# Late modulation pieces on TensorE instead of VectorE, and gathers that pass over padding rows

## The reference, cut to what matters

```python
for layer in range(DEPTH):
    mod_l = jax.nn.silu(c) @ w_ada[layer] + b_ada[layer]        # 6 * 1024 values
    mod_c = jax.nn.silu(c_ctx) @ w_ada[layer] + b_ada[layer]
    sh1, sc1, g1, sh2, sc2, g2 = split(mod_l, 6)
    ...                                                         # mixer gives o_l, o_c
    x_lat = x_lat + g1 * o_l
    f_l = rms_norm(x_lat, g_ffn[layer]) * (1 + sc2) + sh2
    y = moe(f_l, w_router, b_router, w1[layer], w3[layer], w2[layer])
    x_lat = x_lat + g2 * y
```

## Time and profile before

| | us |
|---|---|
| three runs | 3264.39, 3264.18, 3256.47 |
| the profiled execution | 3262.42 |
| its span on the core | 3260.4 |
| TensorE matmul busy | 2899.2 (89%) |
| VectorE busy | 1555.3 (48%) |
| ScalarE busy | 1066.2 (33%) |
| GpSimd busy | 505.9 (16%) |
| mean granted TensorE clock | 0.943 of full |

### The profile page before, as it was taken

The page is one execution under the profiler, slowest core; times in us unless marked ns, Lnnn a source line. Parts: engine busy times, 40 slices in busy tenths (PEclk is TensorE's granted clock), DMA queues, the critical chain, the costliest instruction groups (busy, mean ns, idle before and its releaser), DMA issues. The chain is left out here.

```text
span 3260.4 us, 73070 instructions
## 1 busy us (share of the span) xinstructions
PE 2899.2 (89%) x27907; PEld 1918.0 (59%) x27907; DVE 1555.3 (48%) x4608; ACT 1066.2 (33%) x2418; POOL 505.9 (16%) x802
## 2 busy tenths in 40 slices
PE   6999986889998849999895999899998949997895
PEld 3777743845554437776683455477776526785683
DVE  2333346955557642222223688666666452222223
ACT  1111112456631103333232344355553202332232
POOL 0000002600033012232231000000002003232222
PEclk8999987989999969999997999899999969998998
DMA  9500046500044379999995222200002458999997
GB/s 344 209 26 26 13 182 248 134 1 1 1 144 168 123 312 417 415 417 417 418 400 179 84 91 71 78 1 1 1 1 86 160 226 334 417 416 417 418 416 308
DMA packets 163152, 661.79 MB, mean 203 GB/s; under 512 B 22388, under 2 KB 34852, under 8 KB 113764
## 3 DMA queue, kind: packets, MB, share of 16 engines
q1 hardware_dynamic: 132932, 564.32, 44.0%
q0 software_dynamic: 19424, 63.98, 5.3%
q10 hardware_dynamic: 10560, 30.16, 2.4%
HBM read 576.73 MB, written 81.66 MB: 202 GB/s over the span
## 5 line engine op out<-in xcount | busy, mean ns | idle before, releaser
L2637 PE MATMUL ps_g<-w_ring,work 128*32 128x256 f32 x9632 | 569.8, 384 | 37.5 <-DMA w_ring<-in_w 25.5
L2637 PEld LDWEIGHTS ps_g<-w_ring,work 128*32 128x32 f32 x9632 | 384.8, 111 | 184.7 <-issue 48.3
L2724 DVE STREAM_TRANSPOSE work<-work 128x256 f32<-128x256 f32 x189 | 123.9, 655 | 673.9 <-PE ps_g L2637 656.7
L2690 ACT COPY work<-ps_y 32x256 f32<-32x256 f32 x760 | 276.4, 364 | 285.9 <-PE ps_y L2652 279.1
L2652 PE MATMUL ps_y<-w_ring,work 128*32 128x256 f32 x4896 | 302.1, 380 | 3.3 <-ACT work L2690 3.3
L1771 PE MATMUL of_ps_r<-w_early,cat 128*128 128x512 f32 (+1 forms) x608 | 257.8, 580 | 3.0 <-ACT cat L1854 3.0
L430 PE MATMUL ps_r<-w,hT 128*128 128x512 f32 (+1 forms) x640 | 249.3, 546 | 1.5 <-ACT hT L489 1.5
L2652 PEld LDWEIGHTS ps_y<-w_ring,work 128*32 128x32 f32 x4896 | 202.7, 111 | 70.0 <-ACT work L2690 4.3
L2684 ACT ACTIVATE work<-ps_g 128x128 f32<-128x128 f32 x192 | 53.4, 278 | 542.4 <-PE ps_g L2637 535.8
L2596 POOL DMA_INDIRECT work<-f_dram,ex_idx x200 | 194.7, 974 | 157.4 <-POOL ex_idx L2593 155.9
L1771 PEld LDWEIGHTS of_ps_r<-w_early,cat 128*128 128x128 f32 x608 | 115.7, 194 | 127.1 <-issue 123.5
(11 more groups left out here) (494 smaller groups left out, 4268.0 us busy)
## 6 DMA issues: line engine op xcount, KB each, us to landing
w_ring<-in_w SPq DMA_DIRECT2D x304, 1024.0 KB, 26.5
w_early<-in_w SPq DMA_DIRECT2D x80, 1024.0 KB, 28.0
y_dram<-work ACTq DMA_DIRECT2D x190, 128.0 KB, 5.7
y_dram<-zeros POOLq DMA_DIRECT2D x2, 9216.0 KB, 44.6
ml_staging<-in_w_ada SPq DMA_DIRECT2D x9, 2048.0 KB, 11.9
mo_wa<-in_w_ada SPq DMA_DIRECT2D x6, 2048.0 KB, 9.4
ml_spare<-in_w_ada SPq DMA_DIRECT2D x5, 2048.0 KB, 13.3
ml_arena<-ml_rows SPq DMA_DIRECT2D x40, 256.0 KB, 4.3
```

Of the source, the lines that this page charges most:

```text
L2637: mm = pe.matmul(ps_h[rows, :], xT[:, k * UNIT:(k + 1) * UNIT], w[:, :, kk * DE + n * P:kk * DE + (n + 1) * P], start=k == 0, stop=k == KD ...
L2690: w = act.copy(y[b * UNIT:(b + 1) * UNIT, n * 256:(n + 1) * 256], ps_y[n * UNIT:(n + 1) * UNIT, :])
L2724: dve.transpose(xT.rearrange("p (k t) -> p k t", k=KD), xs.rearrange("p (r k) -> p k r", k=KD)).then_inc(x_turned, 1)
```

## The change

In the mix output of layer 0 the product of piece n moves from VectorE to TensorE: at the end of TensorE's iteration n, behind `router(n - 1)`, TensorE waits for the load of piece n and runs `ada_product` into the free half of `ps_c`. ScalarE copies the row into `M.gate`, rows that GpSimd has used up by then. Behind iteration N - 1 and ahead of `turn_f(N - 1)` TensorE turns all six rows back with 24 matmuls of two columns. VectorE adds the bias for both columns and makes the gain ahead of `scores(N - 2)`. SP's part is not changed: `ada_mm` is still what frees the buffer.

In `route` the values that form the list get an offset: every real entry is the same as before, and a place without a token becomes q - 4, which is negative, for its quarter q. The gather gets a bound (`bounds_check=T * QU - 1`, `oob_is_err=False`), so that such rows are passed over; their places in the tile keep what was there.

```diff
@@ mix_out, TensorE
-                    if 0 < n <= len(M.late):
-                        pe.wait_ge(ada_sum, n)
-                        for m in range(4):
-                            at = P + 4 * (n - 1) + m
-                            mm = pe.matmul(ps_r[:, at:at + 1], wa[:, 0, m * P:(m + 1) * P], g.ones[:, 0:1], start=True, stop=True)
-                        mm.then_inc(ada_mm, 1)
...
                     if n:
                         router(n - 1)
+                    if 0 < n <= len(M.late):
+                        pe.wait_ge(ada_in, 16 * n)
+                        if n > 1:
+                            pe.wait_ge(ada_row, n - 1)
+                        ada_product(pe, g, ps_c[:, 0, :], wa, ada_mm)
+                if M.late:
+                    pe.wait_ge(ada_row, len(M.late))
+                    for j in range(len(M.late)):
+                        for m in range(4):
+                            mm = pe.matmul(ps_c[:, 0, 8 * j + 2 * m:8 * j + 2 * m + 2], M.gate[:, j, m * P:(m + 1) * P], g.pick[:, :], start=True, stop=True)
+                    mm.then_inc(ada_turned, 1)
                 turn_f(N - 1)
@@ mix_out, ScalarE, at the end of iteration n
+                    if 0 < n <= len(M.late):
+                        act.wait_ge(ada_mm, n)
+                        act.wait_ge(normed, n)
+                        act.copy(M.gate[:, n - 1, :], ps_c[:, 0, :]).then_inc(ada_row, 1)
@@ mix_out, VectorE
-                def late(j):
-
-                    dve.wait_ge(ada_in, 16 * (j + 1))
-                    dve.tensor_scalar(wa[:, 0, :], wa[:, 0, :], g.cs[:, 0, 0:1], None, ALU.mult).then_inc(*c.up())
-                    for k in range(1, KD):
-                        own()
-                        w_sum = dve.scalar_tensor_tensor(out=wa[:, 0, :], in0=wa[:, k, :], scalar=g.cs[:, k, 0:1], in1=wa[:, 0, :], op0=ALU.mult, op1=ALU.add)
-                        w_sum.then_inc(*(c.up() if k < KD - 1 else (ada_sum, 1)))
...
-                    if 0 < n <= len(M.late):
-                        late(n - 1)
+                if M.late:
+                    dve.wait_ge(ada_turned, 1)
+                    at = slice(4 * M.late[0], 4 * M.late[-1] + 4)
+                    dve.tensor_tensor(g.mod[:, at, :], ps_c[:, 0, 0:8 * len(M.late)].rearrange("p (a w) -> p a w", w=2),
+                                      g.ba[:, at].unsqueeze(2).to_broadcast([P, 4 * len(M.late), 2]), ALU.add).then_inc(*c.up())
+                    own()
+                    ada_gain(dve, g, 1, 1).then_inc(*c.up())
                 scores(N - 2)
                 scores(N - 1)
@@ route
-    high = R.work[:, LOWS:LOWS + 2 * nt * LISTW]
+    high = R.work[:, 2 * nt * UNIT:2 * nt * (UNIT + LISTW)]
-                                           (tok[:, :], [[4 * P, nt]], 0, 4), (row_no[:, :], [[1, LISTW]], 0, 0)):
+                                           (tok[:, :], [[4 * P, nt]], QU, 4), (row_no[:, :], [[1, LISTW]], 0, 0)):
-            dve.memset(quarter[q * UNIT:(q + 1) * UNIT, :], float(q)).then_inc(*c.up())
+            dve.memset(quarter[q * UNIT:(q + 1) * UNIT, :], float(q - QU)).then_inc(*c.up())
@@ experts, gather
-                                    in_offset=bass.IndirectOffsetOnAxis(idx[:, at:at + 1].bitcast(U32), 0)).then_inc(gathered[at], 16)
+                                    in_offset=bass.IndirectOffsetOnAxis(idx[:, at:at + 1].bitcast(U32), 0),
+                                    bounds_check=T * QU - 1, oob_is_err=False).then_inc(gathered[at], 16)
```

More of the change, by code:

```diff
@@ L1349, in mix_out @@
         r_done, parts_out, l_done, lg_ready, lg_used = s("r_done"), s("parts_out"), s("l_done"), s("lg_ready"), s("lg_used")
-        ada_in, ada_sum, ada_mm = s("ada_in"), s("ada_sum"), s("ada_mm")
+        ada_in, ada_mm, ada_row, ada_turned = s("ada_in"), s("ada_mm"), s("ada_row"), s("ada_turned")
         ps_row = (ps_o[:, :], ps_c[:, :, :].rearrange("p a n -> p (a n)"))
@@ L2298, in route @@
     n, m = nt * NE, nt * NG
+    QU = P // UNIT
     fixed = FIXED
```

## The result

The changed kernel takes 3300.36 us (median of 4 runs, 3299.32 to 3302.13) against 3260.76 us for the kernel before on the same chip (median of 4, 3256.47 to 3264.39): 1.0123 times, interval 1.0105 to 1.014, or 39.6 us slower. The forecast was 3306 us, +43.

| stretch, from mark to mark | before | after | difference | forecast |
|---|---|---|---|---|
| up to output 1 of layer 0's mix output | 965.38 | 963.50 | -1.9 | 0 |
| output 1 to output 8 | 132.84 | 182.10 | +49.3 | +57 |
| output 8 to the first matmul of the routing | 56.33 | 56.99 | +0.7 | -1 |
| from there to the experts' first matmul | 38.79 | 39.68 | +0.9 | 0 |
| experts of layer 0 | 529.15 | 525.21 | -3.9 | -4.9 |

A forecast was written before the change was run, and what follows sets the result against it. TensorE bounds layer 0's mix output; in the experts TensorE and the DMA supply of weights lie close together. Stretch +57, turn -1 and gathers -13 give +43 us, about 3306 us, with a low end of 3291 and a high end of 3328.

The forecast's parts named there:

- The wait: Layer 0's mix output: TensorE waits 9.9 us for each load n = 2 to 6, none for n = 1.
- the rebuilt stretch: Output 1 to output 8 of layer 0's mix output, rebuilt from 16.40 us tiles: 189.8 us for 132.8, +57 us.
- The clock: Layer 0's mix output: lower TensorE clock behind each of five waits costs 2.9 us, between 1.7 and 4.2.
- The products: Layer 0's mix output: six products added to TensorE, 1.85 us each, 11.1 us at full clock, all on the path.
- The turn: End of layer 0's mix output: 48 records, 6.3 us, just fit TensorE's wait for the last `f`; taken as -1 us.
- The gathers: Experts of both layers: passed-over rows give DMA time back, 4.9 and 9.6 us, 14.5 together; 13 us taken.
- GpSimd: Start of each layer's experts, four gathers in a row: the bound's test taken as nothing, between -2 and +4 us.
- A: Experts: passed-over rows bring nothing, 3320 us; chance 0.16.
- B: Experts: gathers bring far more than their share, all 46.0 us of waiting for weights go, 3254 us; chance 0.02.
- C: Layer 0's mix output: whole wait hidden, only the products stay, stretch 125.9 us, 3243 us; chance 0.02.
- D: Experts: each gather gets longer on GpSimd; at +1 us, 3314 us; chance 0.08 together with longer waits.

The follow-up runs named there:

- products alone: The changed kernel with the gathers of before, so only the products have moved: 3315.02 us, 1.0157 times the kernel before.
- gathers alone: The kernel before with only the gathers changed: 3247.52 us, 0.9958 times the kernel before.
- one-tile-later kernel: The changed kernel with each product one iteration later on TensorE, and ScalarE's copy with it: 3243.23 us, 0.9934 times the kernel before.

## Why the prediction was right

The mechanism was right: five waits in the predicted place decide, and the gathers give part back. That the total came out so close, +43 against +39.6, is partly luck: the stretch of the mix output was 7.7 us less than forecast, and the gathers and the turn, each 1.7 us worse, took nearly half of that away again.

*The wait.* Right in place, count and cause: none for the first product, five for the others, each the 0.5 us and the landing. The moved place alone is worth 57 us (3300.36 against 3243.23), as the rebuilt stretch said. The size was a little off: I took the median landing of before, 9.4 us, and it was 8.5 us; the five waits are 45.1 us instead of 49.5.

*The clock.* 2.9 us behind each wait was the price of one earlier case; 11.3 us for five are 2.3 each, inside the bounds 1.7 and 4.2. In each case the product itself ran at the lower clock almost throughout (3.36 to 3.64 us against 1.90); what differs is how much of the next output does (3.70 to 4.87 us for its first eight records). Together with the landing this is the 7.7 us by which +57 was too much.

*The products.* 1.85 us was right; without a wait a tile with a product takes 1.7 us more.

*The turn.* This step failed, by 1.7 us: it fitted the hole only at the full clock, and the clock did not stay up. I had given this case as the worse end of the term. The traces of the other kernels agree: from output 8 to the first matmul of the routing it takes 56.5 to 58.3 us in the seven kernels with the plain turn, 56.3 us in the two without any of this, and 54.6 us where seven wide matmuls kept the clock in its place, which is the gain that I had forecast and more. The size of the loss is within the spread of these traces; that the gain of 1 us did not come is clear of it.

*The gathers.* 13 us taken, 10.9 us measured in the experts. Three terms of that sum were too large. First, I let a passed-over row cost nothing. The DMA views of layer 1's experts, of the kernel before (2690 to 3211 us) and of the one whose gathers there are skipped (2677 to 3176 us), show that q0 keeps a tenth of its share when it moves almost nothing:

```profile
q0 software_dynamic: 4387, 11.98, 6.0%
```

```profile
q0 software_dynamic: 4362, 0.05, 0.6%
```

Second, the rounds. I took 99 and 91 from ScalarE's copies, but TensorE's groups hold 6272 / 64 = 98 and (3360 + 2336) / 64 = 89; ScalarE goes on past the last round. The padding of the rounds is then 18.4% and 28.1%, not 19.2% and 29.7%. Third, the length over which I let the saving count. The windows of the kernel before (us, busy times with their counts, granted clock, DMA share, GB/s) show what I didn't look at, the first two of layer 0 and the third of layer 1:

```profile
1193.00:1243.00 50.00, 48.41 (x860) 31.90 (x864) 14.04 (x37) 13.72 (x40) 16.02 (x31) 0.96 0.74 287
1243.00:1293.00 50.00, 50.00 (x936) 35.95 (x931) 14.76 (x39) 16.29 (x48) 14.72 (x29) 1.00 1.01 415
2690.00:2740.00 50.00, 48.41 (x848) 32.17 (x852) 14.04 (x37) 13.05 (x39) 15.59 (x30) 0.94 0.72 282
```

In the first 50 us of each layer's experts the DMA engines are three quarters busy: the ring has run full during the routing and waits for TensorE. A saving there, I estimate, changes nothing. With the three put right the forecast's own sum is 0.064 x 0.184 x 346 x 0.9 = 3.7 us for layer 0 and 0.064 x 0.281 x 457 x 0.9 = 7.4 us for layer 1, where 3.7 and 7.2 us were measured. This is an estimate made after the result; no run tests the three one by one. Layer 0 of the changed kernel also has two short dips in the DMA rate, to 268 GB/s at 1314 us and to 315 GB/s at 1418 us, together 2.6 us of the full rate against 0.5 us in the kernel before, and layer 1 has none; what they cost the stage isn't shown.

*GpSimd.* I took nothing for the bound. It costs, and can be seen: a gather takes 1024 ns instead of 974, and it is issued 60 ns later. The timeline of GpSimd at the third and fourth of the first gathers, before and after (the same line is L2596 and L2595):

```profile
1189.12 0.98 POOL L2596 DMA_INDIRECT work<-f_dram,ex_idx  x1 [0.79 <-POOL ex_idx L2593]
...
1191.08 0.98 POOL L2596 DMA_INDIRECT work<-f_dram,ex_idx  x1 [0.79 <-POOL ex_idx L2593]
```

```profile
1237.96 1.02 POOL L2595 DMA_INDIRECT work<-f_dram,ex_idx  x1 [0.85 <-POOL ex_idx L2592]
...
1240.03 1.03 POOL L2595 DMA_INDIRECT work<-f_dram,ex_idx  x1 [0.85 <-POOL ex_idx L2592]
```

1.96 us from gather to gather became 2.07. With four in a row at each layer's start that is 0.9 us in all; elsewhere GpSimd has the time (2.07 us and a copy of 0.40, of the 5.2 us that a round takes).

*The rivals.* A (passed-over rows bring nothing) fell with the products alone at 3315 and the gathers alone at 3248; B with the layer whose gathers were skipped. C, as a statement on this kernel, fell with the five waits. It was right as a number for another kernel: with the wait gone it gave 3243 us and 125.9 us for the stretch, and the one-tile-later kernel takes 3243.23 us, 124.9 in the stretch; its runs lie between 3237.75 and 3247.29, so the last digits agree by chance. D exists at 0.1 us a gather.

## What to carry to other kernels

When a product moves from one engine to another, look up in which iteration its input is issued and in which the new engine wants it; an engine that came last in the old chain may have hidden a whole tile of landing time. Here TensorE was given 0.5 us less than nothing for a load of 8.5 us, five times, and one iteration more turned 40 us slower into 17 to 19 us faster, with the same instructions. Rows of a gather that nobody reads were worth 3.7 and 7.2 us here, in stages whose DMA engines are three quarters busy in the first 50 us (shares of 0.74 and 0.72) and full behind them (1.01 in layer 0). That the first 50 us gave nothing is an estimate that fits the two numbers: count the stretch from where the engines are full, not from where the stage begins, and take off the tenth that a passed-over row still cost here.

## What the runs showed of the hardware that I had not expected

Behind 48 matmuls of 128x2, issued without a gap for 7.35 us, the granted clock of TensorE was 0.50, and it fell within them, from 1.00. Behind seven of 128x512 at the same place it was 1.00. An idle time of 3.10 us was followed by the lower clock too (0.52 in the product behind it), those of 0.9 to 1.2 us were not (1.00, and 1.92 us for the product). The changed kernel's five waits of 8.63 to 9.70 us were all followed by the lower clock, which cost 11.3 us together by the sum above.

With the bound, the indirect DMAs moved none of the bytes of the rows they passed over (7.3 MB fewer, of 7.3), while the profile counts as many packets in their queue as before (19424). Of the DMA engines' time in layer 1's experts they gave back nine tenths: 6.0% with all rows read, 0.6% with nearly all passed over.

A load of 1 MB landed in 6.0 us in this stage and one of 2 MB in 8.5 us (medians, without and with the second half).
